# Opening the DeltaNet projections with three weight units per activation tile, with the weight splits, the token mean and the tile steps around it re-ordered

## The reference

```python
x = x + rmsnorm(f, norm_mlp_post[l])                    # end of the first block
h = rmsnorm_2(x, a_norm)                                # start of the second
p = h @ w_in                                            # 1024 x 4112
qkv, gate, b_raw, a_raw = jnp.split(p, [...])           # b_raw, a_raw: 8 columns each, the "tail"
qkv = jax.nn.silu(causal_dwconv(qkv, conv_w))
beta = jax.nn.sigmoid(b_raw)
g = -jnp.exp(A_log) * jax.nn.softplus(a_raw + dt_bias)
o = gated_delta_rule_chunked(q, k, v, beta, g)          # 8 heads, chunks of 64 tokens
```

## Time and profile before

| | |
|---|---|
| median of 3 runs | 1897.49 us (1895.47 to 1900.2) |
| profiled execution, its own time | 1900.44 us |
| its span, first to last instruction | 1898.6 us |
| PE busy | 1873.1 us, 99% |
| DVE busy | 1217.3 us, 64% |
| ACT busy | 790.8 us, 42% |
| POOL busy | 304.5 us, 16% |
| mean granted TensorE clock | 0.996 |

### The profile page before, as it was taken

One profiled execution on the slowest core, in us unless ns is written; L12 is line 12 of the kernel. 1 busy time (PEld: TensorE's weight loads), 2 busy tenths in 40 slices (PEclk: granted clock), 3 DMA queues, 4 the chain that ended last, 5 costly groups with the idle time before them and its releaser, 6 DMA issues.

```text
span 1898.6 us, 29783 instructions
## 1 busy us (share of the span) xinstructions
PE 1873.1 (99%) x10616; PEld 1526.6 (80%) x10616; DVE 1217.3 (64%) x1898; ACT 790.8 (42%) x1491; POOL 304.5 (16%) x225
## 2 busy tenths in 40 slices
PE   9999999999999999999999999999999999999998
PEld 8888888888888767777778888888877888888886
DVE  6997564333333877777746846737778568476474
ACT  5234443233233555555533423424547534243242
POOL 0532232111012300000111100101222211011012
PEclk9999999999999989999999999999999999999999
DMA  5222313232222111111112232222311123222222
GB/s 210 89 100 100 133 68 110 89 106 93 99 89 100 45 56 63 62 62 62 51 56 90 101 121 78 96 104 89 127 70 50 67 89 111 100 88 100 89 101 76
DMA packets 48547, 170.49 MB, mean 90 GB/s; under 512 B 5408, under 2 KB 7616, under 8 KB 48320
## 3 DMA queue, kind: packets, MB, share of 16 engines
q1 hardware_dynamic: 47248, 165.12, 24.9%
q10 hardware_dynamic: 1200, 3.95, 0.6%
HBM read 166.94 MB, written 2.11 MB: 89 GB/s over the span
## 4 chain that ended last, share of the span: by engine, by line
PE 89%; DVE 7%; ACT 2%; issue 1%; POOL 0%; DMA 0%; DVEq 0%; SPq 0%; ACTq 0%; POOLq 0%
PE ps L280 19%; PE ps L282 18%; PE ps L281 17%; PE ps L268 9%; PE ps L269 9%; PE ps L270 9%; PE ps L795 1%; PE ps L820 1%; PE ps L772 1%; DVE scr L1651 1%; DVE scr L1642 1%; DVE Y L1642 1%; ACT Y L1574 0%; DVE scr L1016 0%; PE ps L865 0%
## 5 line engine op out<-in xcount | busy, mean ns | idle before, releaser
L227 ACT ACTIVATE w_hi<-w_raw 128x1024 fp32r<-128x1024 f32 x302 | 315.0, 1051 | 261.5 <-PE ps L282 171.9
L232 DVE TENSOR_TENSOR w_lo<-w_raw,w_hi 128x1024 fp32r<-128x1024 f32 x253 | 343.9, 1362 | 123.0 <-ACT w_hi L227 122.3
L280 PE MATMUL ps<-A_hi,w_hi 128*128 128x512 f32 x882 | 360.8, 409 | 1.9 <-DVE Y L1132 1.1
L282 PE MATMUL ps<-A_hi,w_lo 128*128 128x512 f32 x882 | 345.7, 392 | 0.0
L281 PE MATMUL ps<-A_lo,w_hi 128*128 128x512 f32 x882 | 344.9, 391 | 0.0
L280 PE MATMUL ps<-B_hi,w_hi 128*128 128x512 f32 x680 | 267.9, 394 | 1.3 <-DVE B_lo L1169 0.9
L282 PE MATMUL ps<-B_hi,w_lo 128*128 128x512 f32 x680 | 264.9, 390 | 0.0
L281 PE MATMUL ps<-B_lo,w_hi 128*128 128x512 f32 x680 | 264.6, 389 | 0.0
L280 PEld LDWEIGHTS ps<-A_hi,w_hi 128*128 128x128 f32 x882 | 166.0, 188 | 38.2 <-DVE Y L1132 2.5
L282 PEld LDWEIGHTS ps<-A_hi,w_lo 128*128 128x128 f32 x882 | 166.1, 188 | 35.8
L268 PE MATMUL ps<-A_hi,w_hi 128*128 128x512 f32 x488 | 190.2, 390 | 0.0
(11 more groups left out here) (318 smaller groups left out, 2612.0 us busy)
## 6 DMA issues: line engine op xcount, KB each, us to landing
w_raw<-d_ws SPq DMA_DIRECT2D x304, 512.0 KB, 3.5
X<-d_xT SPq DMA_DIRECT2D x4, 512.0 KB, 7.9
X<-d_xT ACTq DMA_DIRECT2D x1, 2048.0 KB, 8.7
d_out<-X SPq DMA_DIRECT2D x8, 256.0 KB, 2.3
scr<-gc_rows ACTq DMA_DIRECT2D x7, 256.0 KB, 3.1
cst<-d_cst SPq DMA_DIRECT2D x1, 800.0 KB, 12.3
par<-d_par SPq DMA_DIRECT2D x1, 344.5 KB, 3.0
scr<-d_pw SPq DMA_DIRECT2D x1, 256.0 KB, 12.7
```

The source lines that it names most:

```text
L227: nc.scalar.activation(w_hi[:, c], raw[:, c], ACT.Copy).then_inc(S(f"w_hi{s}"), 1)
L232: nc.vector.tensor_tensor(w_lo[:, c], raw[:, c], w_hi[:, c].bitcast(F32), ALU.subtract)\
L280: pe.matmul(ps[bank][:], w_hi[:, c], hi, start=k == 0, stop=False)
L282: last = pe.matmul(ps[bank][:], w_lo[:, c], hi, start=False, stop=k == total - 1)
```

## The change

`second_block_pe` takes three units by tiles instead of two (bank 4 for the third), with the tail between; the token sums are issued ahead of the last tile's matmuls, the spread of the inverse norm right behind the last tile, and the tail's transposes after two blocks of unit 3. The third unit must then be split before the opening: ACT's split of slot 2 goes to the end of the MLP, DVE's ahead of `last_part(1)`. Slot 3 is split by ACT behind tile 3 of `norm_act` and by DVE at the end of `add_normed`. The first two units of the next round are split later, between the tail's arithmetic and the convolution. DVE's token mean goes ahead of the tail copy. The scaled tiles of `add_normed` lie in banks 3 and 2, then 5 and 7, instead of 3 and 4, so that bank 4 is free; `keep_warm` writes bank 0; one wait for the second mean is added. `add_normed` and `keep_warm` are also used at the seam inside the first block.

```diff
@@ norm_act @@
                 square(act, tag, m, tile(X, m))
+                if m in behind:
+                    behind[m]()
@@ second_block_pe @@
             for k in range(KT):
+                if k == KT - 1:
+                    token_sums(pe, "na", KT, 2)
                 pe.wait_ge(S("na_hi"), count("na_hi", k + 1))
-                for s in range(2):
+                for s in range(3):
                     open_hi(pe, rnd(U_DELTA, 0), s, pairA, k, 4)
...
                 pe.wait_ge(S("na_lo"), count("na_lo", k + 1))
-                for s in range(2):
+                last = pe.matmul(ps[6][0:16, :], TW[0][:, c], lo, start=False, stop=k == KT - 1)
+                if k == KT - 1:
+                    last.then_inc(S("tail"), 1)
+                for s in range(3):
                     open_lo(pe, s, pairA, k, 4)
-                last = pe.matmul(ps[6][0:16, :], TW[0][:, c], lo, start=False, stop=k == KT - 1)
-            last.then_inc(S("tail"), 1)
-            token_sums(pe, "na", KT, 2)
-            open_segment(pe, rnd(U_DELTA, 0), 2, pairA, 0, 3, wait_na, 4)
+            open_row(pe, "na")
+            open_segment(pe, rnd(U_DELTA, 0), 3, pairA, 0, 2, wait_na, 4)
             pe.wait_ge(S("tail_copy"), count("tail_copy", 1))
...
-            open_segment(pe, rnd(U_DELTA, 0), 2, pairA, 3, 6, wait_na, 4)
-            open_row(pe, "na")
-            open_segment(pe, rnd(U_DELTA, 0), 2, pairA, 6, KT, wait_na, 4)
-            open_segment(pe, rnd(U_DELTA, 0), 3, pairA, 0, KT, wait_na, 4)
+            open_segment(pe, rnd(U_DELTA, 0), 3, pairA, 2, KT, wait_na, 4)
@@ second_block_act @@
-            for k in range(2):
-                ahead(act, split_hi, rnd(U_DELTA, 0), k)
-            norm_act(act, "na", "a_norm", pairA, "post1", "x2")
-            for k in range(2, SLOTS):
-                ahead(act, split_hi, rnd(U_DELTA, 0), k)
+            norm_act(act, "na", "a_norm", pairA, "post1", "x2",
+                     behind={3: lambda: ahead(act, split_hi, rnd(U_DELTA, 0), 1)})
...
             a.activation(BETA, BETA, ACT.Tanh, scale=0.5).then_inc(S("g_act"), 1)
+            ahead(act, split_hi, rnd(U_DELTA, 0), 2)
             act.wait_ge(S("g_act"), count("g_act", 2))
             a.activation(Z2, Z2, ACT.Ln, bias=1.0).then_inc(S("g_act"), 1)
             conv_act(act, 0, 0)
+            ahead(act, split_hi, rnd(U_DELTA, 0), 3)
             conv_act(act, 0, 1)
@@ second_block_dve @@
+            token_mean(dve, "na", 2, D)
             dve.wait_ge(S("tail"), count("tail", 1))
             v.tensor_copy(DT[0:16, :], ps[6][0:16, :]).then_inc(S("tail_copy"), 1)
-            token_mean(dve, "na", 2, D)
-            for k in range(1, SLOTS):
-                ahead(dve, split_lo, rnd(U_DELTA, 0), k)
...
             conv0(1, 0)
+            ahead(dve, split_lo, rnd(U_DELTA, 0), 2)
             dve.wait_ge(S("g_act"), count("g_act", 4))
...
             conv0(0, 4)
+            ahead(dve, split_lo, rnd(U_DELTA, 0), 3)
             conv0(1, 1, 2, 3)
@@ tensor, after norm_pe of post0 and of post1 @@
-            keep_warm(pe, 8)
+            keep_warm(pe, 8, 0)
@@ scalar, last unit of the MLP @@
                         if last and 4 * i + k == KT - 1:
+                            ahead(act, split_hi, rnd(U_DELTA, 0), 0)
@@ add_normed @@
-                    tmp = of(ps[3 + m % 2][:])
+                    tmp = of(ps[3 - m if m < 2 else 5 + 2 * (m % 2)][:])
...
                             mean(1)
+                            dve.wait_ge(S(tag + "_ms"), count(tag + "_ms", 2))
@@ vector, end of the MLP @@
             post1_mean(0)
+            ahead(dve, split_lo, rnd(U_DELTA, 0), 0)
             last_part(1)
             add_normed("post1", "x2", "mlp_post", "na", "a_norm", post1_mean)
-            ahead(dve, split_lo, rnd(U_DELTA, 0), 0)
+            ahead(dve, split_lo, rnd(U_DELTA, 0), 1)
             second_block_dve(dve)
```

More of the change, by code:

```diff
@@ L444, in first_sum_squares, with norm_act @@
                     .then_inc(S("n0_ss"), 1)
-        def norm_act(act, tag, g, pair, post, xtag):
+        def norm_act(act, tag, g, pair, post, xtag, behind={}):
             def row_copy(side):
```

## The result

The changed kernel takes **1900.45 us** (median of 22 runs, 1899.67 to 1901.14). The kernel before, in as many runs, takes 1897.38 us (1895.38 to 1900.29). The ratio is 1.0015, with a 95% interval from 1.0009 to 1.0021: slower by 3 us, and inside the 0.3% that was called no change. The spreads differ more than the medians. That of the kernel before is 4.9 us wide, that of the changed one 1.5 us, and it lies at the slow end of the other. All 22 executions of the changed kernel have a mean granted clock of 0.997, like the profiled one. Those of the kernel before, in the 33 runs beside the first experiments, have 0.996 to 0.999, the low ones where the time is long.

The account below looks back on a forecast made before the run. DVE's list, with ACT's table load and tanh, was taken to bound the seam; 1900.44 + 3.3 (late chain) + 2.6 (new clock fall) - 4.3 (old fall gone) = 1902.0; forecast 1901.5 us, range 1898 to 1905.

Parts of the forecast that it names:

- PE's part: Opening to end of unit 3: 12 matmuls per tile remove PE's small waits; 1.5 us gained for PE alone.
- The early splits: Slots 2 and 3 split ahead, into idle time: no cost; POOL's power may grow 1.3 us, bound 0.5 us.
- The chain: DVE's list from the tail's arithmetic to head 0's transposes: 3.3 us late, bounds 1.8 to 3.8.
- Item 1: Tail's arithmetic on DVE: waits for PE's later tail transposes, starting at 645.8 instead of 644.94, +0.85 us.
- Item 2: ACT between tanh and table load: a split of 1.05 us put there delays DVE's restart by 0.95 us.
- Item 3: Between the taps of units 0 and 1: ACT's new split, then DVE's, delay unit 1's taps by 1.5 us.
- The clock: TensorE's clock falls in the new 5.3 us wait, +2.6 us; the old fall ahead of the inversion goes, -4.3.
- The half-length case: Behind the new wait before head 0's transposes: low clock lasting half as long costs +0.8 instead of +2.6, giving 1900.2.
- The sum: Whole kernel: +3.3 +2.6 -4.3 = +1.6 on the profiled 1900.44 us, giving 1902.0.
- The rival with a second fall: Clock falls again ahead of the inversion, so the 4.3 us stay: 1904.5 to 1906.3 us; chance 0.27.
- No fall at all: Clock holds through PE's 5.3 us wait: 1899.4 us, or 1903.7 with the late fall alone; chance 0.12.
- The rival that it works as its words say: At the seam, splits find their holes, waits shrink and the fall at 669 goes: 1894.6 us; chance 0.10.

Follow-up runs that it names:

- b_banks: Kernel before with only the change's small parts (other banks for scaled tiles and filler, added wait for the second mean): 1897.42 us, ratio 0.9997.
- a_move3: Changed kernel with only the split of slot 1 moved later, behind unit 1's tanh (ACT) and the evacuations of units 2 and 3 (DVE): 1898.44 us.
- a_holes: Changed kernel with both late splits (slots 0 and 1) moved into idle time further ahead, PE's order as changed: 1897.68 us, ratio 1.0002.
- a_fill2: Changed kernel with 20 filler matmuls ahead of head 0's transposes and eight ahead of the inversion's first step: 1899.82 us, ratio 1.0007.
- b_fill: Kernel before with eight small filler matmuls in the 2.03 us wait ahead of head 0's inversion: 1896.19 us, ratio 0.9992.
- a_fill1: Changed kernel with 20 filler matmuls in its 5.1 us wait ahead of head 0's transposes: 1901.48 us, ratio 1.0016.
- b_best0: Kernel before, PE's two units by tiles kept, with early splits, mean, tail copy and row, DVE's late splits moved into waits: 1894.63 us, ratio 0.9984.

## Why the prediction was right

**PE's part.** Right. The last tile was to end 23.1 us behind the opening (643.6); it ends at 642.77 - 619.71 = 23.06, where the next four small matmuls begin. The wait for `g_tok` was forecast at 0.6 and is 0.72.

**The early splits.** Right, at no cost. POOL's power grew from 0.71 to 1.62 us beside DVE's split, 0.9 and not 1.3, and the opening is as far behind it as before (6.23 us, was 6.24). PE did wait a little for it: the matmuls that spread side 0's power start 0.32 us behind the last ones of side 1, where they started 0.12 behind, and the filler gave those 0.2 back (4.88 us from there to the opening, was 4.89). The forecast had them at nothing for that reason. Its growth of 1.3 compared a power of 128x2 with one of 128x4, which takes 1.02 us without a split beside it. b_banks confirms the zero for banks and wait.

**The chain.** Right in each item, with sizes from the profile, against the earlier trace rows. Item 1, the tail's lateness: forecast 0.85, measured 1.06. Item 2, ACT's split ahead of the table load: 0.95, measured 0.95. Item 3, the split ahead of unit 1's taps: 1.5, measured 1.48. Together 3.3, measured 3.48. a_move3 takes out item 3 and gets 1.48 back, and a_holes leaves item 1, 1.05, and 0.31 of its own second split. The bounds of 1.8 to 3.8 hold it, and a_fill2 against b_fill, both without a fall in their profiles, gives 3.63 us in whole execution times.

**The clock.** The mechanism was right and one term was mis-sized. The fall came in the long wait, the wait ahead of the inversion shrank from 2.03 to 0.78 and no second fall followed. The 4.3 us that the old fall cost came back as 4.0 (30.42 to 26.41); the third of a microsecond in front was too much. The new fall was sized at 2.6 and costs 0.83: the step that failed is "if it stays low for about as long". The forecast let 10.1 us of low clock begin where PE resumes. Measured are 6.8 us, of which 2.35 lie in the wait, so that PE works at half speed for 4.45 us. That makes it some 2.2 us slower (half of 4.45, an estimate), and 1.25 of this go into the wait ahead of the inversion (2.03 before, 0.78 now). The half-length case, "+0.8", came true in size; why the low stretch is shorter than before no run shows.

**The sum.** From the profile before, forecast +1.6. At the seam, the three distances add up to 78.43 us after and 78.13 before: +0.30, and the difference is the clock's term. (The profiled execution itself, 1899.88 us, is 0.56 faster than the one before, mostly because its opening comes 0.78 us earlier.) Against the median it is otherwise: the kernel before has the full cost of the fall only in some executions, and the changed one has its small cost, as far as its spread and its mean clock of 0.997 tell, in all. The level without a fall was put at 1896.1; b_fill measures 1896.19. With 3.48 and 0.83 this gives 1900.5, and 1900.45 was measured. That the two agree to 0.1 us is partly luck: in the set of b_fill the kernel before ran at 1898.17, 0.8 us above its 1897.38 here, and b_fill itself still spreads over 2.3 us. The forecast of 1901.5 lay between the case that came and the one that did not.

The rival with a second fall did not come in the changed kernel. a_fill1 shows half of it: with the first wait filled there is one fall, the late one, which the forecast had at 1903.7 under "No fall at all"; its three slowest executions take 1903.76 to 1904.69 us. The profile of a_holes has the same pattern without filler: the clock holds behind a wait of 3.62 us and falls at the next. The rival that it works as its words say fails at items 1 to 3. b_best0 gets the gain with PE's old order and other places for the splits; the new order with an early tail was not run.

What stays open: why one wait of about 2 us, or one of 3.6, is followed by a fall in one execution and not in the next (b_banks and the kernel before, a_holes and a_move3), and what sets the length of the low stretch.

## What to carry to other kernels

Giving PE more work per tile fills small waits only; if it puts off a small result that another engine's long chain starts from (here 16 columns for DVE), the wait comes back at the end of that chain, and larger. Work that is moved out of one list's busy stretch has to land where that engine waits: the same two splits cost 2.4 us of the chain in the changed kernel and 0.3 in a_holes. When a kernel's times spread over some microseconds, look for a stretch at the lower clock behind a wait of PE, and try cheap matmuls in that wait. Look at the next wait too: filling only the first one made the changed kernel slower (a_fill1), since the slower PE had been covering the second.

## What was not expected of the hardware

The wait of 5.08 us costs less than that of 2.03: 0.83 against 4.0 us. The low stretch is shorter, 6.8 us against 10.2 (669.05 to 679.3 in the kernel before), 2.35 us of it pass while PE waits, and the next wait takes up another 1.25.

Neither the length of the wait nor the kind of matmuls behind it tells how long the clock stays low. Behind waits of 2.03 to 2.05 us, with the same matmuls of 64 and 512 columns following, it was low for 10.2 us (the kernel before, a_holes), for 6.8 us (a_fill1, 673.3 to 680.1) and not at all (b_banks); the stage took 30.4, 29.3 and 26.4 us. Behind 1.44 us it was low for 3.4 us (b_best0), and behind 3.61 us for 3.4 us as well (a_move3). So one kernel's times can spread over 4 us and more although no instruction changes.
